# The joint between the last expert group and the first feed-forward: order of weight halving, squares, mean and outputs

## The reference, cut to what matters

```
x = x + g2 * expert_choice_ffn(...)              # last layer of the first block
h = x
h = h + 0.5 * swiglu(rms_norm_2(h, ffn1_norm[0]), w_gate, w_up, w_down)
rms_norm_2(x, g) = x * rsqrt(mean(x*x) + 1e-6) * g
swiglu(x)        = (silu(x @ w_gate) * (x @ w_up)) @ w_down      # 1024 -> 2816 -> 1024
```

## Time and profile before

| | us |
|---|---|
| median of 3 runs | 2356.39 (2355.3 to 2364.88) |
| profiled execution, its own time | 2363.0 |
| its span, first to last instruction | 2360.4 |
| TensorE busy | 2098.8 (89%) |
| VectorE busy | 1111.1 (47%) |
| ScalarE busy | 839.0 (36%) |
| GpSimd busy | 44.0 (2%) |

### The profile page before, as it was taken

One profiled execution on the slowest core, in us unless ns is written; L12 is line 12 of the kernel. 1 busy time (PEld: TensorE's weight loads), 2 busy tenths in 40 slices (PEclk: granted clock), 3 DMA queues, 4 the chain that ended last, 5 costly groups with the idle time before them and its releaser, 6 DMA issues.

```text
span 2360.4 us, 31724 instructions
## 1 busy us (share of the span) xinstructions
PE 2098.8 (89%) x13615; PEld 1472.0 (62%) x13615; DVE 1111.1 (47%) x1695; ACT 839.0 (36%) x1234; POOL 44.0 (2%) x76
## 2 busy tenths in 40 slices
PE   9999999879787999856655669999999999999998
PEld 5865753324232777523322238888988888888887
DVE  5646541102010677301010118768877677657765
ACT  4336321001000556200000016544655465456544
POOL 0022000000000011000000000000000000000000
PEclk9999999999999999978787879999999999999999
DMA  8276579999999453899999994454444554354442
GB/s 354 110 316 250 214 324 428 427 428 427 428 428 426 198 227 127 334 428 425 428 426 428 427 421 179 161 194 175 178 188 161 190 203 179 134 226 185 156 170 89
DMA packets 66827, 660.85 MB, mean 280 GB/s; under 512 B 7488, under 2 KB 10560, under 8 KB 21120
## 3 DMA queue, kind: packets, MB, share of 16 engines
q1 hardware_dynamic: 66688, 658.83, 68.4%
HBM read 657.76 MB, written 1.05 MB: 279 GB/s over the span
## 4 chain that ended last, share of the span: by engine, by line
PE 66%; DMA 27%; DVE 3%; ACT 2%; issue 1%; SPq 0%; DVEq 0%; ACTq 0%
PE ps L957 21%; PE ps L958 10%; PE ps L1455 9%; DMA ring<-in_exp_up 9%; DMA ring<-in_exp_gate 8%; PE ps L927 5%; PE ps L928 5%; PE ps L929 5%; DMA ring_top<-in_exp_up 4%; DMA ring<-in_exp_down 4%; PE ps L1448 2%; PE ps L976 2%; DMA ring<-in_ada_w 1%; PE ps L1144 1%; DMA ring_top<-in_exp_down 1%
## 5 line engine op out<-in xcount | busy, mean ns | idle before, releaser
L1455 PE MATMUL ps<-ring,arena 128*32 128x256 f32 (+1 forms) x1776 | 229.8, 524 | 89.0 <-DMA ring<-in_exp_up 48.1
L957 PE MATMUL ps<-h_buf_r,ring_r 128*128 128x512 f32 x832 | 295.3, 399 | 2.9 <-DVE h_buf_r L755 2.9
L2793 DVE TENSOR_TENSOR h_buf<-h_buf,ps 128x512 f32<-128x512 f32 (+1 forms) x32 | 17.7, 554 | 511.1 <-PE ps L1455 499.7
L1455 PEld LDWEIGHTS ps<-ring,arena 128*32 128x32 f32 (+1 forms) x1776 | 84.5, 135 | 231.5 <-issue 93.9
L958 PE MATMUL ps<-h_buf_r,ring_r 128*128 128x256 f32 x800 | 224.7, 281 | 0.0
L1455 PE MATMUL ps<-ring_top,arena 128*32 128x256 f32 (+1 forms) x1200 | 159.2, 520 | 69.5 <-DMA ring_top<-in_exp_gate 37.7
L957 PE MATMUL ps<-h_buf_r,ring_top_r 128*128 128x512 f32 x576 | 204.4, 399 | 1.1 <-DVE h_buf_r L755 1.1
L486 DVE TENSOR_TENSOR ring_r<-ring,ring_r 128x2048 fp32r<-128x2048 f32 (+4 forms) x88 | 174.1, 2015 | 39.5 <-ACT ring_r L478 39.4
L957 PEld LDWEIGHTS ps<-h_buf_r,ring_r 128*128 128x128 f32 x832 | 156.4, 188 | 41.9 <-issue 3.0
L958 PE MATMUL ps<-h_buf_r,ring_top_r 128*128 128x256 f32 x608 | 170.8, 281 | 0.0
L1455 PEld LDWEIGHTS ps<-ring_top,arena 128*32 128x32 f32 (+1 forms) x1200 | 57.0, 132 | 169.1 <-issue 66.2
(11 more groups left out here) (382 smaller groups left out, 4167.2 us busy)
## 6 DMA issues: line engine op xcount, KB each, us to landing
ring<-in_exp_gate SPq DMA_DIRECT2D x38, 2048.0 KB, 28.7
ring<-in_exp_up SPq DMA_DIRECT2D x35, 2048.0 KB, 30.5
ring<-in_exp_down SPq DMA_DIRECT2D x33, 2048.0 KB, 30.4
ring_top<-in_exp_down SPq DMA_DIRECT2D x27, 2048.0 KB, 30.5
ring_top<-in_exp_gate SPq DMA_DIRECT2D x26, 2048.0 KB, 30.5
ring<-in_ffn_w SPq DMA_DIRECT2D x50, 1024.0 KB, 6.8
ring_top<-in_exp_up SPq DMA_DIRECT2D x24, 2048.0 KB, 30.5
ring_top<-in_ffn_w SPq DMA_DIRECT2D x38, 1024.0 KB, 6.8
```

Of the source, the lines that this page charges most:

```text
L957: release(pe.matmul(ps[:, bank, :], w[0][:, lo:lo + P], both, start=start, stop=False, skip_group_check=True))
L1455: mm = pe.matmul(out, stationary, slot(c)[:, at:at + width], start=start, stop=stop)
```

## The change

Chunk 0 of the first feed-forward is halved in four quarters (`steps_of` 4; w_out's first chunks keep their four). VectorE takes, for each tile: its addition, behind every other addition a quarter of the weights, and the rest of the tile before. ScalarE halves a quarter after leads 0, 2 and 4, and halves chunk 1 before it squares. The six additions of squares are issued by GpSimd. The last group's eight outputs go to banks 0 to 3, two to a bank, and an addition waits until both outputs of its bank are written. TensorE no longer waits for four additions of the last group at chunk 0; it waits for all eight ahead of chunk 1. In the first feed-forward the mean products stand in chunk 1, ahead of t = 2, directly before the wait for the root. `halved_for` is written for any number of pieces. The other three feed-forwards keep their order.

```diff
@@ -421,8 +421,8 @@
                 parts_of[expert_chunk(l, EXPERTS - 1) + c] = 2
 
         steps_of = list(parts_of)
-        for l in range(LAYERS):
-            steps_of[chunk_at["w_out", l]] = 4
+        for n in (chunk_at["w_out", 0], chunk_at["w_out", 1], chunk_at["ffn", 0]):
+            steps_of[n] = 4
 
         home_of = {chunk_at[name, l] + c: (name, l, c) for name, l, c in HOMES}
 
...
@@ -491,6 +491,22 @@
 
         def keys(q):
             return (0, 512) if q < 2 else (256, 256)
+
+        def squares(i):
+
+            if i == 3:
+                return part(0, 2048).rearrange("p (k t) -> p k t", k=KT)
+            return part(0, 4096).rearrange("p (k t) -> p k t", k=KT) if i < 4 else \
+                part(2560, 4608).rearrange("p (k t) -> p k t", k=KT)
+
+        def add_square(eng, i, d, order=range(KT)):
+
+            if d in (0, KT - 1):
+                return
+            eng.wait_ge(sem("norm_squares"), KT * i + d + 1)
+            sums = squares(i)[:, order[0], :] if d == 1 else sq_sum
+            eng.tensor_tensor(sq_sum, sums, squares(i)[:, order[d], :], ALU.add).then_inc(sem("square_added"), 1)
+            eng.wait_ge(sem("square_added"), (KT - 2) * (i - 2 * LAYERS) + d)
 
         block = ctx.enter_context(nc.Block())
 
...
@@ -690,12 +706,9 @@
                     pool.tensor_scalar(q_band[:, u % 8, :], qk_t[:, h // 2, P * q:P * q + P],
                                        band[:, h % 2:h % 2 + 1], None, ALU.mult).then_inc(sem("d_bands"), 1)
 
-        def squares(i):
-
-            if i == 3:
-                return part(0, 2048).rearrange("p (k t) -> p k t", k=KT)
-            return part(0, 4096).rearrange("p (k t) -> p k t", k=KT) if i < 4 else \
-                part(2560, 4608).rearrange("p (k t) -> p k t", k=KT)
+            for d in range(KT):
+                add_square(pool, 2 * LAYERS, d)
+
 
         def norm_pe(pe, release, i):
             width = 2 * N if i == 0 else N
...
@@ -907,9 +911,11 @@
             return [(o_lat[rows_, width * q:width * q + width], ps[CAP * q:CAP * q + CAP, 3, 0:width])
                     for q in (2 * half, 2 * half + 1)]
 
-        def moe_bank(l, g, d):
-
-            return (4 + d) % 8 if l and g == 3 else 4 + d % 4
+        def moe_out(l, g, d, s):
+
+            if l and g == 3:
+                return ps[:, d // 2, N * (d % 2):N * (d % 2) + N]
+            return ps[:, 4 + d % 4, N * s:N * s + N]
 
 
         @block.tensor
...
@@ -948,8 +954,8 @@
             def halved_for(n, k, tiles):
 
 
-                if k in (0, tiles // 2):
-                    halved_chunk(n, k and 1)
+                if k * steps_of[n] % tiles == 0:
+                    halved_chunk(n, k * steps_of[n] // tiles)
 
             def wide(bank, w, lo, both, start, stop):
 
...
@@ -1442,10 +1448,10 @@
                 streams = 2 if l == 0 else 1
                 pe.wait_ge(sem("o_read"), 2 * (4 * g + 4) + before("o_read", l))
                 for d in range(KT):
-                    if KT * g + d >= 4 and moe_bank(l, g, d) >= 4:
+                    if KT * g + d >= 4 and not (l and g == 3):
                         pe.wait_ge(sem("moe_added"), KT * g + d - 3 + before("moe_added", l))
                     for s in range(streams):
-                        mm = pe.matmul(ps[:, moe_bank(l, g, d), N * s:N * s + N], (o_lat, o_ctx)[s][:, P * d:P * d + P],
+                        mm = pe.matmul(moe_out(l, g, d, s), (o_lat, o_ctx)[s][:, P * d:P * d + P],
                                        scatter(l)[:, s, g, :], start=True, stop=True)
                     mm.then_inc(sem("moe_out"), 1)
 
...
@@ -1535,7 +1541,7 @@
             def ffn(i, norm):
                 n = chunk_at["ffn", i]
                 if i == 0:
-                    pe.wait_ge(sem("moe_added"), LAST_GROUP + 4 + before("moe_added", 1))
+                    pe.wait_ge(sem("moe_added"), LAST_GROUP + before("moe_added", 1))
                 elif i == 1:
                     pe.wait_ge(sem("lru_added"), 4)
                 elif i == 2:
...
@@ -1556,6 +1562,10 @@
                         for t in range(4):
                             if c >= 2 and t % 2 == 0:
                                 pe.wait_ge(sem("ffn_products_read"), 2 * (PAIRED * i + c - 2) + t // 2 + 1)
+                            if c == 1 and t == 0 and i == 0:
+                                pe.wait_ge(sem("moe_added"), LAST_GROUP + KT + before("moe_added", 1))
+                            if c == 1 and t == 2 and i == 0:
+                                norm_mean(pe, release, norm)
                             if c == 1 and t == 2:
                                 pe.wait_ge(sem("norm_std"), norm + 1)
                             for k in range(KT):
...
@@ -1565,7 +1575,7 @@
                             if t % 2:
                                 mm.then_inc(sem("ffn_products"), 1)
                     owed[0] += 1
-                    if c == 0:
+                    if c == 0 and i:
                         norm_mean(pe, release, norm)
                 late = FT - 2
                 for d, lo, hi in [(0, 0, late), (1, 0, late), (0, late, FT), (1, late, FT)] + [(d, 0, FT) for d in range(2, KT)]:
...
@@ -2326,11 +2336,11 @@
             for d in range(KT):
                 act.wait_ge(sem("moe_added"), start + d + 1)
                 lead(act, d, gain)
-                if d == 1:
-                    halve_lead(act, n, 1)
+                if d in (0, 2, 4):
+                    halve_lead(act, n, d // 2 + 1)
+            halve_lead(act, n + 1)
             for d in range(KT):
                 square(act, 2 * LAYERS, d)
-            halve_lead(act, n + 1)
             f = [chunk_at["ffn", i] for i in range(2 * LAYERS)]
             ffn(0, 4, norm_gain("mix_norm", 0), (chunk_at["lru", 0], chunk_at["lru", 0] + 1))
             lru()
...
@@ -2772,11 +2782,11 @@
             def moe_add(l, g, tiles=range(KT)):
 
                 for d in tiles:
-                    dve.wait_ge(sem("moe_out"), KT * g + d + 1 + before("moe_out", l))
+                    written = d + 1 + (1 - d % 2 if l and g == 3 else 0)
+                    dve.wait_ge(sem("moe_out"), KT * g + written + before("moe_out", l))
                     for s in range(2 if l == 0 else 1):
                         x = x_res[:, d, N * s:N * s + N]
-                        ins = dve.scalar_tensor_tensor(x, ps[:, moe_bank(l, g, d), N * s:N * s + N], mod[:, l, 5 * KT + d, s:s + 1], x,
-                                                       ALU.mult, ALU.add)
+                        ins = dve.scalar_tensor_tensor(x, moe_out(l, g, d, s), mod[:, l, 5 * KT + d, s:s + 1], x, ALU.mult, ALU.add)
                     ins.then_inc(sem("moe_added"), 1)
 
             def experts(l):
...
@@ -3135,18 +3145,13 @@
                 if l == 0:
                     halve_rest(dve, chunk_at["w_in", 1], 0)
             n, gain = chunk_at["ffn", 0], norm_gain("ffn1_norm", 0)
-            moe_add(1, 3, range(4))
-            halve_rest(dve, n, 0)
-            for d in range(2):
-                rest(dve, 4, d, gain)
-            moe_add(1, 3, range(4, KT))
-            for d in (2, 3):
-                rest(dve, 4, d, gain)
-            halve_rest(dve, n, 1)
-            for d in range(4, KT):
-                rest(dve, 4, d, gain)
-            for d in range(KT):
-                add_square(dve, 4, d)
+            for d in range(KT + 1):
+                if d < KT:
+                    moe_add(1, 3, (d,))
+                if d % 2 == 0 and d < KT:
+                    halve_rest(dve, n, d // 2)
+                if d:
+                    rest(dve, 4, d - 1, gain)
             halve_rest(dve, n + 1)
             f = [chunk_at["ffn", i] for i in range(2 * LAYERS)]
             ffn(0, 4, norm_gain("mix_norm", 0), (chunk_at["lru", 0], chunk_at["lru", 0] + 1))
```

More of the change, by code:

```diff
@@ L756, in rest @@
                                      ALU.mult, ALU.subtract).then_inc(sem("norm_halved"), 1)
-        def add_square(dve, i, d, order=range(KT)):
-            if d in (0, KT - 1):
-                return
-            dve.wait_ge(sem("norm_squares"), KT * i + d + 1)
-            sums = squares(i)[:, order[0], :] if d == 1 else sq_sum
-            dve.tensor_tensor(sq_sum, sums, squares(i)[:, order[d], :], ALU.add).then_inc(sem("square_added"), 1)
-            dve.wait_ge(sem("square_added"), (KT - 2) * (i - 2 * LAYERS) + d)
         def norm_gain(name, l):
```

## The result

| | median us | runs |
|---|---|---|
| before | 2360.98 (2352.5 to 2364.88) | 22 |
| changed | 2363.39 (2357.95 to 2371.08) | 22 |

The ratio is 1.0021, with an interval of 1.0011 to 1.003: 5.0 us more, between 2.6 and 7.1. The forecast was 2360.7 against a median of 2356.39, 4.3 more. The base itself came out 4.6 higher with more runs, so the two medians lie only 2.4 apart and the ratio is what to go by. The profiled execution of the changed kernel happens to be the fastest of its 22 (2357.95, span 2356.1), so its span says nothing of the change. The joint has to be read by itself.

What follows compares the result with a forecast made beforehand. From the joint on TensorE was taken as the bound, so shifts there count fully. Chunk 2 starting at S + 10.3 (S = 1430.6) against 1436.62 costs +4.3 us; on the median 2356.39 that gives 2360.7, range 2354.8 to 2367.0.

Steps and rivals of the forecast that it cites:

- Start of the first product: First feed-forward, chunk 0: TensorE goes straight on from the scatter at 1411.91 instead of 1413.01, gaining 1.1 us.
- Chunk 1's weights: ScalarE copies them before the squares, so TensorE's half-chunk wait moves from 1426.62 to 1425.4: gain 1.2 us, containing the 1.1.
- GpSimd: Six dependent additions of squares before the mean, taken as 1.18 us each, 7.1 in all, ending at 1430.5.
- the rival of the held port: GpSimd's additions can't run beside VectorE's halving of chunk 1 and start only at 1425.35: cost +6.2, chance 0.2.
- +3.3: Total cost in us given with the Trainium skill's estimate of 0.56 us per GpSimd addition, called the low end's.
- the floor's +3.4: Cost in us if GpSimd's additions end early and half of chunk 1 sets S at 1429.7.
- S: Start of the mean products in the first feed-forward, forecast at 1430.6 against 1424.18 before.
- The mean and the root: Wait for the root directly behind the mean in chunk 1: TensorE may go on at S + 1.6.
- The queue behind the root: Copy, halving, reciprocal, reading of chunk 0's gates: chunk 2 starts at S + 10.3, not S + 7.3, a 3.0 us stall.
- The sum: Whole effect at the start of chunk 2: cost S - 1426.3, which with S = 1430.6 is +4.3 us.
- The clock falls in the new stall: Granted clock drops to 0.50 for some 3 us after the stall before chunk 2: about 1.5 more, +5.8; chance 0.05.
- The other side, a start that is kept: Chunk 0's gates are read before TensorE is ready for chunk 2, keeping the early start: 2355.2 to 2356; chance 0.12.

Runs made afterwards that it cites:

- e2: Kernel before with only the first feed-forward's mean products moved ahead of t = 2 of chunk 1; ratio to before 1.0034, joint 33.52 us.
- e6: Changed kernel with squares ahead of chunk 1's copy, additions on VectorE and mean behind chunk 0, as in before; ratio to before 1.0009, joint 31.71 us.
- e11: Changed kernel with additions of squares on VectorE and ScalarE's copy of chunk 2's weights ahead of the root; ratio to before 1.0003, joint 30.78 us.
- e7: Changed kernel with additions on VectorE, chunk 2's copy ahead of the root, and mean in the middle of t = 1; ratio to before 0.9989.
- e9: The kernel e7 run again, unchanged; ratio to before 1.0006, joint 30.09 us.
- e10: The kernel e7 with ScalarE's copy of chunk 2's weights back behind the root; ratio to before 1.0014, joint 32.46 us.
- e1: Kernel before run again without an edit, for a second trace; joint 30.47 us.
- e4: Changed kernel with the six additions of squares on VectorE again, behind chunk 1's halving; ratio to before 1.0026, joint 33.46 us.
- e3: Changed kernel with ScalarE's copy of chunk 2's weights ahead of the root in the first feed-forward; ratio to before 1.0034, joint 36.75 us.
- e5: Changed kernel with the mean back behind chunk 0, squares still late and additions on GpSimd; ratio to before 1.0024, joint 38.32 us.
- e8: The kernel e7 with chunk 1 halved in quarters too; ratio to before 1.001, joint 30.27 us.

## Why the prediction was right, step by step

- **Start of the first product.** Forecast: 1.1 gained, straight behind the scatter at 5.95. The start did move, but with a fast scatter the limit was VectorE's rest of tile 0 (0.48 of idle time): 4.20 behind the scatter's first product, against about 5.3 for before's order at that clock (e2). The gain of 1.1 was right at equal clocks (1.06), but for another reason than the forecast's. The forecast's reason holds for a slow scatter: in e6 to e11, with this front, the first product follows the scatter with no wait. One wait had no place in the forecast: ScalarE's first quarter began 1.12 late, since the DMA of chunk 0's weights landed only then (1404.88).
- **Chunk 1's weights.** The second half of chunk 1's first gate tile was expected to start 1.2 earlier in the joint (at 19.4 in place of 20.7). It started at 18.73 (1422.66), and in e2, also with a fast scatter, at 18.87. With slow scatters it is 19.19 in each of e7, e9, e10 and e11, which have this part of the change, against 20.66 in before and e1. So the term is worth 1.5 with a slow scatter, near the 1.2, and only 0.14 with a fast one, since a fast scatter brings 1.8 to the order of before and 0.5 to this one. The forecast had not asked what the scatter's clock does to it.
- **GpSimd.** Taken as 1.18 each, 7.1 for six. An addition takes 0.73 alone; the first took 2.63, of which 1.9 fit a wait until VectorE's halving was over (1422.6). Six took 6.69. Size nearly right from two wrong parts, which is luck: a price that was too high, and the rival of the held port, which came true for one addition. The estimate of 0.56 that the prediction made from the Trainium skill (GPSIMD Engine Reference, "Elementwise — side-by-side cycle accounting") is nearer to the measured 0.73 than my choice; the +3.3 given with it should have been the floor's +3.4. The additions were to put S 0.9 behind the end of half of chunk 1; they put it 0.23 behind. S came 23.4 behind the scatter's first product, in place of 24.6: the squares were ready 0.8 sooner than forecast, and the additions took 0.4 less.
- **The mean and the root.** S + 1.6 until TensorE goes on: 1429.01 - 1427.32 = 1.69. Right.
- **The queue behind the root.** S + 10.3 was forecast and 10.41 measured; the stall 3.0 was forecast and 2.80 measured. e2, e10 and e11 show that it is this queue: it is there with the mean late and gone with the copy ahead.
- **The sum.** +4.3 was forecast, +5.0 (2.6 to 7.1) measured. The joint shows +3.1 to +3.3 with unequal scatters. At equal clocks it is more: about +5.0 with both fast (33.80 against the estimated 28.8), and about +3.7 with both slow (33.80 and the 0.46 by which this order is later behind a slow scatter, against 30.57). Both are estimates, since neither kernel was traced with the other's scatter. The forecast lies between them. That it comes within 1 us of the measured total is partly chance, as the interval is 4.5 us wide; and the clock adds to the cost in some executions, as follows.
- **The rivals.** "The clock falls in the new stall" had 0.05 and was argued against from one later pause. In the changed kernel's trace the clock stays at 1.00 around the stall, but in e2 and e4, whose stalls are as long, it does not. The rows of e4, then those of the changed kernel:

```profile
1438.00:1440.00 2.00, 0.22 (x1) 0.22 (x2) 1.93 (x3) 0.00 (x0) 0.00 (x0) 1.00 0.00 0
1440.00:1442.00 2.00, 2.00 (x8) 1.67 (x8) 1.75 (x3) 0.69 (x2) 0.00 (x0) 0.57 0.29 57
1442.00:1444.00 2.00, 2.00 (x9) 1.76 (x8) 0.69 (x1) 2.00 (x2) 0.00 (x0) 0.58 0.90 369
```

```profile
1436.00:1438.00 2.00, 0.27 (x1) 0.27 (x2) 1.93 (x3) 0.00 (x0) 0.00 (x0) 1.00 0.00 0
1438.00:1440.00 2.00, 2.00 (x13) 1.72 (x13) 1.70 (x3) 0.74 (x2) 0.00 (x0) 1.00 0.31 53
```

In e4 the first four microseconds behind the stall hold 17 matmuls, in the changed kernel 13 in two: 9 missing at 6.5 per us, or 1.4 us lost in such an execution. One row of one pause was too little to give this 0.05, all the more as the very pause of the earlier trace rows is followed by the lower clock in six of the thirteen traces, the changed kernel's among them (shown in the last section). The other side, a start that is kept, would have needed the reading 3.0 us sooner; it was not.

## What to carry to other kernels

When a step that feeds several engines is moved later, do not ask only whether its direct consumer can wait. Follow what is queued behind that consumer on its engine, and on the next one, to the resource that the first engine wants back: here a 0.5 us root carried 9 us of copy, halving and reciprocal on its back, although both engines were idle ahead of it. And work given to GpSimd was only cheap here while VectorE did not read two SBUF inputs at that time: a cure that is right by itself (e3) can fail on this, and succeed once the additions are back on VectorE (e11).

## What the runs showed of the hardware that was not expected

**One program, two paces.** Executions differ in how far apart the pairs of a 512- and a 256-column matmul start, with the granted clock at 1.00 throughout. The window 1440 to 1530 us of before and of e1, the same program:

```profile
1440.00:1530.00 90.00, 90.00 (x511) 78.05 (x510) 67.39 (x62) 49.22 (x54) 0.00 (x0) 1.00 0.45 170
```

```profile
1440.00:1530.00 90.00, 90.00 (x522) 78.69 (x521) 68.64 (x64) 51.06 (x55) 0.00 (x0) 1.00 0.46 180
```

That is 511 matmuls against 522 in equal time. A wide matmul reads 395/398/403 ns in the first and 392/392/395 in the second, and a chunk of 32 pairs takes 11.31 and 11.09 us. Averaged over 120 us or more between two pauses, the pairs start 0.3467 or 0.3533 us apart, one or the other, in each of the thirteen traces. Where the pace changes, it does so near 1440, 1700, 1920 or 2120 us, the places where TensorE pauses or goes over to other products; between them it is kept. About 700 us of the rest of the kernel go in such pairs, and 1.9% of that is 13 us, more than twice the effect studied here. From chunk 2 to the end before took 923.8 (2360.4 - 1436.62), e1 918.7 and e7 913.9, with the same work. What sets the pace is open; no run was made for it. It may be a reason why medians of before moved between 2356.54 and 2360.98 from one group of runs to the next, which is not shown. In the traces of e7 and e9, one and the same kernel, the joints are alike (29.96 and 30.09), and from chunk 2 to the end they took 913.9 and 921.7: e7 keeps 0.3467 up to 2120, e9 has 0.3533 up to there.

**One pause, two outcomes for the clock.** Ahead of chunk 2 the granted clock fell to its lower level with the stalls of e2 (2.81 us) and e4 (2.88) and did not with those of the changed kernel (2.80) and e10 (2.42). It also fell with the waits of 3.98 in e3 and 7.29 in e5. All thirteen traces have one more pause in common, the 2.9 us wait of the earlier trace rows, 2.86 to 2.88 long in each. The granted clock fell there in six (e1, the changed kernel, e3, e4, e9, e11) and stayed at 1.00 in seven (before, e2, e5, e6, e7, e8, e10). Before and e1 are one program, and so are e7 and e9, and each pair has both outcomes. The first matmul behind the pause, and two windows of 2 us from there, in before and in the changed kernel:

```profile
1927.22 0.47 PE L957 MATMUL ps<-h_buf_r,ring_r 128*128 128x512 f32 x1 [2.87 <-DVE h_buf_r L755]
...
1927.00:1929.00 2.00, 1.78 (x10) 1.58 (x11) 1.97 (x7) 2.00 (x6) 0.00 (x0) 1.00 0.28 41
1929.00:1931.00 2.00, 2.00 (x13) 1.76 (x12) 1.97 (x6) 2.00 (x4) 0.00 (x0) 1.00 0.75 307
```

```profile
1928.27 0.77 PE L963 MATMUL ps<-h_buf_r,ring_r 128*128 128x512 f32 x1 [2.86 <-DVE h_buf_r L768]
...
1928.00:1930.00 2.00, 1.73 (x5) 1.57 (x6) 1.97 (x6) 2.00 (x6) 0.00 (x0) 0.51 0.00 0
1930.00:1932.00 2.00, 2.00 (x9) 1.67 (x9) 2.00 (x6) 2.00 (x4) 0.00 (x0) 0.64 0.86 274
```

That is 23 matmuls against 14 in about four microseconds. So the cost of a stall of this length differs from one execution to the next by more than a microsecond, with the kernel unchanged. These traces do not say what decides it.
